# Gated-delta heads of a two-layer mixer: the next head's convolutions, sigmoids and squares inside the current head's recurrence, and output tiles that wait for their bank's readers

## The reference

```
qkv = silu(centred_dwconv(concat([qa, ka, va]), conv))    # 5 taps along the tokens
q, k = l2norm(q), l2norm(k);  g = -exp(a_log) * softplus(ga + bias);  beta = sigmoid(ba)
o_f, s_f = gdn_chunked(q, k, v, g[0], beta[0], s0[:, 0])              # forward
o_b, s_b = gdn_chunked(flip(q), ..., beta[1], s0[:, 1])               # backward
out = rmsnorm(o_f + flip(o_b)) * silu(za)

gdn_chunked:  t = inverse(I + strict_lower(kb @ k.T * decay))         # per chunk
              u = t @ vb;  w = t @ (kb * exp(g))
step over chunks:  v_new = u - w @ s;  o = q_dec @ s + (q @ k.T * decay) @ v_new
                   s = s * exp(g_last) + k_dec.T @ v_new
```

## Time and profile before

| | us |
|---|---|
| median of three runs | 3170.83 |
| lowest and highest run | 3168.66, 3173.48 |
| the profiled execution, its own time | 3164.74 |
| its span in the trace | 3162.8 |
| PE, DVE, ACT, POOL busy in the span | 2956.2, 1602.9, 821.4, 2083.2 |

### The profile page before, as it was taken

The page is one execution under the profiler, slowest core; times in us unless marked ns, Lnnn a source line. Parts: engine busy times, 40 slices in busy tenths (PEclk is TensorE's granted clock), DMA queues, the critical chain, the costliest instruction groups (busy, mean ns, idle before and its releaser), DMA issues. The chain is left out here.

```text
span 3162.8 us, 63199 instructions
## 1 busy us (share of the span) xinstructions
PE 2956.2 (93%) x26338; PEld 2742.0 (87%) x26338; DVE 1602.9 (51%) x3166; ACT 821.4 (26%) x1666; POOL 2083.2 (66%) x2491
## 2 busy tenths in 40 slices
PE   7999989999999999999979989989999999999996
PEld 2698879899999988889968888979999998887996
DVE  1655665556664534457654755673665511444112
ACT  2432334211112223320043442332111222333000
POOL 4475455477778774458857555455777888453886
PEclk9999999999999999999989999999999999999998
DMA  9421121144553421135531211122554322112223
GB/s 406 155 87 53 39 67 64 37 127 135 147 136 120 148 86 42 41 136 174 188 137 62 67 61 51 42 66 76 147 147 126 94 73 70 47 47 70 82 75 116
DMA packets 112558, 319.82 MB, mean 101 GB/s; under 512 B 16976, under 2 KB 30416, under 8 KB 111120
## 3 DMA queue, kind: packets, MB, share of 16 engines
q1 hardware_dynamic: 81536, 263.38, 26.4%
q10 hardware_dynamic: 30736, 52.40, 4.8%
HBM read 302.65 MB, written 13.08 MB: 100 GB/s over the span
## 5 line engine op out<-in xcount | busy, mean ns | idle before, releaser
L556 POOL TENSOR_SCALAR w_hi<-raw 128x256 fp32r<-128x256 f32 x1216 | 1067.4, 903 | 1009.7 <-PE projection L663 531.6
L563 POOL TENSOR_TENSOR w_lo<-raw,w_hi 128x256 fp32r<-128x256 f32 x1232 | 965.6, 814 | 6.3 <-ACT w_hi L1185 6.3
L661 PE MATMUL projection<-h_hi,w_hi 128*128 128x320 f32 x2304 | 741.8, 322 | 10.4 <-POOLq L568 4.5
L662 PE MATMUL projection<-h_lo,w_hi 128*128 128x320 f32 x2304 | 712.8, 309 | 1.1 <-issue 1.1
L663 PE MATMUL projection<-h_hi,w_lo 128*128 128x320 f32 x2304 | 712.8, 309 | 0.0
L603 PE MATMUL projection<-h_hi,w_hi 128*128 128x320 f32 x1984 | 618.5, 312 | 22.4 <-POOLq L568 20.0
L605 PE MATMUL projection<-h_hi,w_lo 128*128 128x320 f32 x1984 | 613.7, 309 | 0.0
L604 PE MATMUL projection<-h_lo,w_hi 128*128 128x320 f32 x1984 | 613.5, 309 | 0.0
L661 PEld LDWEIGHTS projection<-h_hi,w_hi 128*128 128x128 f32 x2304 | 435.3, 189 | 17.9 <-issue 9.1
L662 PEld LDWEIGHTS projection<-h_lo,w_hi 128*128 128x128 f32 x2304 | 435.4, 189 | 1.6 <-issue 1.6
L663 PEld LDWEIGHTS projection<-h_hi,w_lo 128*128 128x128 f32 x2304 | 434.4, 189 | 0.0
(11 more groups left out here) (411 smaller groups left out, 4402.9 us busy)
## 6 DMA issues: line engine op xcount, KB each, us to landing
raw<-in_w_stream SPq DMA_DIRECT2D x308, 512.0 KB, 3.6
mod_weights<-in_w_mod SPq DMA_DIRECT2D x160, 384.0 KB, 3.1
work<-in_w_ada SPq DMA_DIRECT2D x37, 512.0 KB, 6.8
work<-rows ACTq DMA_DIRECT2D x32, 320.0 KB, 4.6
xo<-rows ACTq DMA_DIRECT2D x32, 320.0 KB, 5.0
aux<-in_w_ada SPq DMA_DIRECT2D x18, 512.0 KB, 6.8
xo<-in_x ACTq DMA_DIRECT2D x1, 5120.0 KB, 18.1
work<-in_x ACTq DMA_DIRECT2D x16, 320.0 KB, 4.9
```

What stands on the lines that cost most here:

```text
L556: nc.gpsimd.tensor_scalar(w_hi[:, s, cs, :], raw[:, s, cs, :], 1.0, None, ALU.mult).then_inc(split_part, 1)
L563: nc.gpsimd.tensor_tensor(w_lo[:, s, cs, :], raw[:, s, cs, :], w_hi[:, s, cs, :].bitcast(F32), ALU.subtract).then_inc(split_part, 1)
L661: mm(o, w_hi[:, half, c, :], h_hi[:, k, hs], start=(k == 0), stop=False)
L662: mm(o, w_hi[:, half, c, :], h_lo[:, k, hs], start=False, stop=False)
```

## The change

The front of a head gets a stage of its own, `s_frt`, with its own semaphores: F is the front of the head at work, G that of the next one. PE, ACT and DVE issue parts of G inside the current head's recurrence. For the first head of a layer the front stands ahead of the head as before, with k first instead of q. "k sum" of the next head now stands between the last state products and "o sum"; "q sum" behind "k turned"; v is turned in `wb`. `pads` move into `aux`, a buffer that no other work uses by then, and `convs` and the squares to other rows of `work`. The taps read their weights in the parameters, and the copy of them (`hcw`) goes. Bodies of all but the last head of a layer end with `B.leave`, which waits for nothing. Five of a head's six input loads are issued in the head before, behind the square of o; that of `row_beta[0]` behind "q rstd". The takes of the first two tiles move behind the column scaling, z's sigmoid behind the decays, and "z ready" behind the masks' products. The numbers of cells come from `GDN_CELLS`, its first row for the first head of a layer, its second for the other three; what is left of the 64 follows "o sum". In the output projection the second tile waits for "taken1" of the turn before instead of "begun". The core of the diff:

```diff
+GDN_CELLS = ((3, 1, 2, 1, 1, 2, 2, 1, 2, 1, 1, 2), (0, 1, 2, 1, 2, 7, 2, 2, 3, 2, 2, 2))
...
-        pads = [flat(9, PADW), flat(11, PADW), flat(13, PADW)]
-        convs = [flat(15, CONVW), flat(10, CONVW, xo), flat(7, CONVW)]
+        pads = [aux[:, i * PADW:(i + 1) * PADW] for i in range(3)]
+        convs = [flat(2, CONVW), flat(6, CONVW), flat(6, CONVW)]
+        Q_SQ, K_SQ, O_SQ = wt(13), wt(15), wt(14)
...
+        s_frt = stage("gdn_front")
...
+                        if k == 0 and j < 2 and self.before:
+                            self.before.wait("act", f"ahead taken{j + 2}")
...
-                    ahead.cells(16)
-                    B.wait("act", "q squared")
-                    B.did(column_sums(wa, wt(9)), "q sum")
-                    ahead.cells(1)
-                    B.wait("act", "k squared")
-                    B.did(column_sums(wb, wt(11)), "k sum")
-                    ahead.cells(4)
-                    B.wait("dve", "k normed")
+                    if h == 0:
+                        ahead.cells(16)
+                        F.wait("act", "k squared")
+                        F.did(column_sums(wb, K_SQ), "k sum")
+                    ahead.cells(gaps[0])
+                    F.wait("dve", "k normed")
                     B.did(transposed(wb, wt(1)), "k turned")
-                    ahead.cells(2)
-                    B.wait("dve", "v silu")
-                    B.wait("act", "q rstd")
-                    B.did(transposed(wa, wt(4)), "v turned")
-                    ahead.cells(2)
+                    ahead.cells(gaps[1])
+                    F.wait("act", "q squared")
+                    if before:
+                        before.wait("act", "o rstd")
+                    F.did(column_sums(wa, Q_SQ), "q sum")
+                    F.leave()
+                    ahead.cells(gaps[2])
+                    F.wait("dve", "v silu")
+                    B.wait("act", "k turned taken")
+                    B.did(transposed(wb, wt(3)), "v turned")
+                    ahead.cells(gaps[3])
+                    F.wait("act", "q rstd")
+                    B.did(each_tile(wa, wt(1), wt(1)), "kk")
+                    ahead.cells(gaps[4])
                     B.wait("act", "v turned taken")
-                    B.did(each_tile(wa, wt(1), wt(1)), "kk")
-                    B.wait("dve", "q normed")
+                    F.wait("dve", "q normed")
                     B.did(each_tile(wb, wt(1), wt(0)), "qk")
-                    ahead.cells(9)
+                    ahead.cells(gaps[5])
...
-                        ahead.cells(1)
+                        ahead.cells(gaps[11])
+                    ahead.cells(2)
+                    B.wait("dve", f"o taken1{TILES - 1}")
+                    if G:
+                        G.wait("act", "k squared")
+                        G.did(column_sums(wb, K_SQ), "k sum")
+                    ahead.cells(1)
+                    B.wait("dve", f"o taken0{TILES - 1}")
+                    B.wait("act", "o squared")
+                    B.did(column_sums(wa, O_SQ), "o sum")
                     ahead.finish()
...
-                    B.wait("dve", "begun")
+                    if before:
+                        before.wait("dve", "taken1")
...
+                def head_inputs(h):
+                    for d in range(2):
+                        act.dma_start(gdn_state(d), io["state_gdn"][l, d, h, :, :]).then_inc(state_in[d], 16)
+                        row(h, d, row_g[d], 0, rows_in)
+                    row(h, 1, row_beta[1], 1, beta_in)
...
+                    rsqrt(F, Q_RSTD, wa[:, 0:TOK], Q_RSTD, 1.0, "q rstd", DK_SCALE)
+                    F.wait("dve", "v silu")
+                    F.leave()
+                    row(h, 0, row_beta[0], 1, beta_in)
...
+                        if n == 2:
+                            take(B, n0_, 2, xt(6))
+                        if G and n == 2:
+                            conv_sigmoid(G, 1)
+                        if G and n == 3:
+                            B.wait("act", "ahead taken2")
+                            padded(G, 2)
+                            squared_of(G, 1)
+                        if G and n == 4:
+                            conv_sigmoid(G, 0)
+                    B.wait("dve", "o whole")
+                    B.did(A(O_SQ, wt(4), ACT.Square), "o squared")
+                    if G:
+                        head_inputs(h + 1)
+                        G.wait("pe", "k sum")
+                        rsqrt(G, K_RSTD, wb[:, 0:TOK], K_RSTD, 1.0, "k rstd")
+                    B.wait("pe", "o sum")
+                    rsqrt(B, O_RSTD, wa[:, 0:TOK], O_RSTD, 1.0 / P, "o rstd")
+                    if G:
+                        conv_sigmoid(G, 2)
+                        squared_of(G, 0)
+                    B.wait("dve", "z ready")
                     take(B, n0_, 3, xt(7))
...
+                        if d == 0:
+                            F.wait("act", "q rstd")
+                            F.did(tt(wt(0), wt(0), Q_RSTD, ALU.mult), "q normed")
+                            F.leave()
...
+                        dve.wait_ge(beta_in[d], (l * H_A + h + 1) * 16)
...
+                    B.wait("act", "z sigmoid")
+                    B.link(tt(xt(8), xt(7), xt(9), ALU.mult), "z ready")
+                    if G:
+                        zeros(G)
...
+                        if G and n == 0:
+                            B.wait("pe", "wT1")
+                            taps(G, h + 1, 1, range(0, 3))
+                        if G and n == 1:
+                            taps(G, h + 1, 1, range(3, CONV_K))
+                            B.wait("act", "kdec1")
+                            taps(G, h + 1, 0, range(0, 1))
+                        if G and n == 2:
+                            taps(G, h + 1, 0, range(1, 4))
+                        if G and n == 3:
+                            taps(G, h + 1, 0, range(4, CONV_K))
+                            silu(G, 1, wt(1))
+                            taps(G, h + 1, 2, range(0, 1))
                     B.did(V.memset(cst[:, 2:3], 0.0), "o whole")
+                    if G:
+                        taps(G, h + 1, 2, range(1, CONV_K))
+                        silu(G, 0, wt(0))
+                        k_normed(G)
                     B.wait("act", "o rstd")
...
+                    if G:
+                        silu(G, 2, wt(3))
+                        B.leave()
```

More of the change, by code:

```diff
@@ L826, in _ @@
                                   f"ld{d}{v}")
-                        ahead.cells(1)
+                        ahead.cells(gaps[6])
                         for d in range(2):
@@ L852, in _ @@
                         B.did(each_tile((wa, wb)[d], KBG[d], INV_T[d]), f"wT{d}")
-                    ahead.cells(2)
+                    ahead.cells(gaps[10])
                     B.wait("act", "vb1")
@@ L1133, in _ @@
                     B.leave()
+                    before = B
                 B = s_res.body("pe", pe, l)
@@ L1275, in _, with padded, conv_sigmoid, squared_of @@
                 B.end()
+                def padded(F, i):
+                    F.wait("dve", "zeros")
+                    F.did(A(pads[i][:, 2:2 + CTX], xt(4 + i)[:, 0:CTX], ACT.Copy))
+                    F.did(A(pads[i][:, 6 + CTX:6 + TOK], xt(4 + i)[:, CTX:TOK], ACT.Copy), f"{'qkv'[i]} padded")
+                def conv_sigmoid(F, i):
+                    F.wait("dve", f"{'qkv'[i]} conv")
+                    sigmoid(F, pads[i][:, 0:CONVW], convs[i], f"{'qkv'[i]} sigmoid")
+                def squared_of(F, i):
+                    F.wait("dve", f"{'qk'[i]} silu")
+                    F.did(A((Q_SQ, K_SQ)[i], wt(i), ACT.Square), f"{'qk'[i]} squared")
@@ L1278, in _ @@
+                padded(F, 0)
+                padded(F, 1)
+                head_inputs(0)
+                conv_sigmoid(F, 1)
+                padded(F, 2)
+                squared_of(F, 1)
+                conv_sigmoid(F, 0)
+                F.wait("pe", "k sum")
+                rsqrt(F, K_RSTD, wb[:, 0:TOK], K_RSTD, 1.0, "k rstd")
+                conv_sigmoid(F, 2)
+                squared_of(F, 0)
+                before = None
                 for h in range(0, H_A):
                     B = s_gdn.body("act", act, l * H_A + h)
-                    now = int((l * H_A + h + 1) * 16)
+                    G = s_frt.body("act", act, l * H_A + h + 1) if h + 1 < H_A else None
@@ L1289, in _ @@
-                    for tile, kind in ((row_g[0], 0), (row_beta[0], 1)):
-                        act.dma_start(tile, rows[kind, bass.ds(h, 1), :].partition_broadcast(P)).then_inc(rows_in[0], 16)
-                    for i in range(2):
-                        B.wait("dve", f"{'qk'[i]} conv")
-                        sigmoid(B, pads[i][:, 0:CONVW], convs[i], f"{'qk'[i]} sigmoid")
-                        if i == 0:
-                            sigmoid(B, xt(9), xt(7), "z sigmoid")
-                    B.wait("dve", "q silu")
@@ L1297, in _ @@
```

(31 more changed lines are left out.)

149 lines of the change are left out of this document (76 added, 73 removed).

## The result

The changed kernel takes **3126.91 us** in the median of four runs (3123.91 to 3131.30), the kernel before 3172.12 beside it (3168.66 to 3173.48): a ratio of 0.9864, 95% interval 0.985 to 0.9878. The profiled executions stand 40.8 us apart (3164.74 and 3123.91), with a span of 3122.3 after. The forecast was 3145, a gain of 26: the sign and the whole range (3118 to 3168) held, the size did not, and the forecast's own range (3131 to 3159) was left at its fast end.

A forecast was written before the change was run, and what follows sets the result against it. PE was taken as the bound, with 85.5 us in eight GDN heads not work; 59 would remain, a gain of 26: 3138.7 us profiled, 3145 as median. Range 3118 to 3168, the forecast's own 3131 to 3159.

The forecast's parts named there:

- left alone: PE idle time in the GDN heads, mostly issue in the block products, that the change would not touch: 29.4 us.
- masks, all heads: PE waiting for DVE's masks before the first block product: 0.6 us in later heads, 6 in each layer's first.
- k normed and k's square in the first heads: Front of a layer's first head: PE stalls 1.9 us for k normed.
- copy of v_new for the fifth step: Recurrence: ACT's copy comes 0.7 us late, behind k's silu and square, in three heads of a layer.
- k normed and q's square in the second heads: Counted as for any later head: k normed hidden with 2.7 us to spare, q's square hidden by 0.5.
- ends of the fourth heads: End of a layer's fourth head: PE finishes its cells and waits 1.1 us for the last take.
- the forecast's clock: PE's clock falling behind the long mask stall in a layer's first head: 2 us added for each.
- rival 3: Larger gain: block-product issue idle shrinks by a third, first heads wait 2 us without a clock fall: 3123; chance 0.20.
- q stall: PE's wait for ACT's square before q's sum, 3.9 us each, would go in six heads.
- o stall: PE's 1.5 us wait for ACT's square before o's sum would go in six heads.
- Rival 1: DVE bounds the recurrence because moved taps wait for POOL, 1.7 us a tap: slower, 3187 us; chance 0.10.
- Rival 2: The stall only moves to the masks in every head, 3.6 us instead of 0.6: 3175, no change; chance 0.13.

The follow-up runs named there:

- experiment 1: Changed kernel with ten cells of each later head moved from the block levels to ahead of the masks: 3158.12 us, 0.9963 of the kernel before.
- experiment 2: Kernel before, front unmoved, with four cells a block level instead of two, taken from ahead of the masks and behind the blocks: 3201.32 us, ratio 1.0103.
- experiment 9: Kernel of experiment 8 with two cells a recurrence step, the freed cells in the block levels, and k squared behind the fifth step's copies: 3094.26 us.
- experiment 7: Changed kernel with two cells a recurrence step instead of three, except in a layer's first head; five cells go ahead of the masks: 3121.41 us.
- experiment 8: Changed kernel; z product and zeros behind first block level, first heads' five cells ahead of masks with early take, q squared before v's sigmoid: 3114.64, then 3110.32 us.

## Why the prediction was right, and where it was not

The bound and the place were right: all but 0.7 us of the change is idle time and busy time in the GDN heads. The sum, term by term, over both layers:

| term | forecast us | measured us |
|---|---|---|
| left alone (issue and small waits) | 29.4 | 13.9 |
| masks, all heads | 3.6 + 12 | 17.2 |
| k normed and k's square in the first heads | 3.8 | 3.5 |
| copy of v_new for the fifth step | 4.2 | 0 |
| k normed and q's square in the second heads | 0 | 6.1 |
| ends of the fourth heads | 2.2 | 1.9 |
| busy time over 98.8 a head (the forecast's clock) | 4 | 3.2 |
| sum | 59.2 | 45.8 |

The waits are those shown, with 0.4 us for k's square in one first head from the same view; the 4.4 for k normed (line L699) are 0.53 and 2.57 in the two first heads and 0.63 in each second one. The last term is 793.6 less 8 x 98.8. "Left alone" is the rest of the 42.6 us: 8.5 issue, 3.9 in the whole-tile levels, which no term of the forecast held, and 1.5 of small waits. The 17.2 for the masks hold the 4.0 of the second direction; its 3.0 before lay in the 29.4.

**The step that failed** is "29.4 left alone": mostly issue in the block products "which the change leaves alone", and its other form, "the cells moved into blocks and levels only space them", costed at nothing. With the spacing, issue fell by 16 us (24.6 to 8.5), more than the 13 by which the sum missed. Experiments 1, 2 and 9 show it from both sides. The other 5 of the 18 us between 3145 and 3126.91 are some 1.5 of rounding and of time outside the heads, and the step from the profiled execution to the median, put at 6.3 and measured as 3.0. The row that could have told me stood in the earlier trace rows: issue waits of up to 2.6 us lay in the densest stretch of small products, and I named no cause for them, so what four cells between them would do entered only as a chance: it is in rival 3, as a third less, 10 us, at 0.20.

**Right.** The q stall and the o stall are gone from six heads save where a second head lacks cells. The first heads' 6 us for the masks came at 5.88 and 4.38, the later heads' 0.6 at 0.75 in four of six, with 0.71 more in each for the second direction, which I had not counted. The step of the recurrence is 4.86 (4.85 forecast). The ends cost 0.9 each (1.1). The output tiles cost nothing. The second and third heads are 99 to 104 us long from one "q sum" to the next (103 to 105 forecast); that the shorter ones owe it to the issue time is argued, not shown head by head. The clock fell round the first heads' stall.

**Wrong in size.** The copy of v_new was to be 0.7 us late; it ended in time, but only just. In the fifth step ACT's first copy runs to 496.44 by its row, the second to 496.60, and PE begins at 496.55, without idle time, with the product that needs the first. No row stood behind the 0.3 us that the forecast adds for a semaphore; with two cells a step, where PE does wait (0.89, experiment 7), it begins 0.05 us after the end of the copy:

```profile
496.18 0.26 ACT L1400 ACTIVATE work<-wa 128x128 f32<-128x128 f32 x1
496.33 0.27 ACT L1400 ACTIVATE xo<-wb 128x128 f32<-128x128 f32 x1
...
496.55 0.43 PE L897 MATMUL wa<-work 128*128 128x128 f32 x2
```

```profile
495.51 0.26 ACT L1400 ACTIVATE work<-wa 128x128 f32<-128x128 f32 x1
...
495.82 0.49 PE L897 MATMUL wa<-work 128*128 128x128 f32 x2 [0.89 <-ACT work L1400]
```

**Missed.** I counted four cells behind "o sum" for every later head. A layer's first head spends all its 64 cells earlier and leaves none, so the second head reaches its "q sum" 3.5 us sooner, and q's square, hidden by 0.5 in my count, is late: 2.39 us in each layer. Squaring q ahead of v's sigmoid removed that wait (experiment 8). k normed, with 2.7 to spare in my count, is late by 0.63 in the same heads, which fits the same 3.5 us.

**The rivals.** Rival 1 falls: the taps after are

```profile
L1821 DVE SCALAR_TENSOR_TENSOR work<-aux,parameters,work x96: 885/903/1256, 195.4 to 2027.7; 128x644 f32<-128x644 f32 x96
```

with the median and the maximum of the earlier trace rows, though they now lie in the recurrence beside POOL, and experiment 7 leaves DVE in time even in a step of 3.97. The rule of the Trainium skill, SBUF — State Buffer, "Who interferes with whom", would have the later of the two wait out the earlier in full; no tap here took the 1.7 us of that. On POOL's side the stretch of the recurrence after (480.00 to 499.70) has 0.92 us an operation (9.20 in 10) where the earlier trace rows has 0.76; whether that is such a wait is not shown. Rival 2 holds in the first heads alone. Rival 3 gave 3123, near the result, but by two halves of which one was right: issue shrank, by two thirds and not one, while the first heads did wait 4 to 6 us and the clock did fall. That the total comes out near it is luck.

## What to carry to other kernels

Work that a serial chain no longer needs as its cover is worth as much for where it can stand next as for the wait that it leaves: cost the new place of every filler instruction, and the gaps that it breaks up. Before idle time is called left alone, find what ends it: "issue" in a dense stretch of small instructions is a resource too. And when cells are moved forward in an order, ask which later bank, take or queue they bring forward with them.

## What the runs showed of the hardware

I had not expected what the issue gaps are. One of them in the kernel before, PE in order of time, and the DMA queues in a window of 1.2 us inside it (packets, MB, share):

```profile
566.83 0.32 PE L685 MATMUL wb<-xo,work 128*32 128x32 f32 x15
569.74 0.39 PE L685 MATMUL wb<-xo,work 128*32 128x32 f32 x23 [2.60 <-issue]
```

```profile
q8 instruction: 1, 0.02, 4.9%
```

PE stops in the middle of forty equal products; a packet of the queue q8, which the profile calls an instruction queue, is under way in the gap and ends 1.29 us before PE goes on. Over its whole span this queue moves 207 packets:

```profile
q8 instruction: 207, 3.39, 0.4%
```

That is 16 KB each, and 52,676 matmuls and weight loads of the earlier trace rows make some 254 for each packet. In the trace of the kernel before, the stretches of over 0.25 us in which neither matmul nor weight load ran ahead of the block products fall into two kinds: 22, of 24.2 us in all, end 1.24 to 1.56 us after the end of such a packet; of the 16 others, the waits for the masks, one ends 1.72 us after a packet and the rest 2.6 us or more. In the changed kernel the first kind counts 10, of 8.2 us. The gap shown is the longest; in 20 of the 22 the packet had already ended when PE stopped, by up to 1.2 us, so what is common to them is the 1.24 to 1.56 us between the packet's end and PE's start. The reading is that in the block products, where packets mostly follow each other by 3.3 to 4.3 us, PE runs out of instructions, and that with cells of 0.88 us for twelve instructions between them it does so less. That the packet is the cause is inferred from these times and from experiments 1, 2 and 9, which change the spacing; no run changed the queue itself.

Such a gap costs more than its own length. Behind the one shown the granted clock is low, and so it is behind the longest that is left in the changed kernel, of 1.83 us; round the wait of 2.39 us for q's square in that kernel it is not (columns as in the earlier trace rows, the first of the kernel before, the others of the changed one):

```profile
569.70:574.00 4.30, 4.26 (x113) 3.82 (x114) 2.00 (x4) 0.00 (x0) 0.00 (x0) 0.60 0.01 4
```

```profile
1976.54 0.26 PE L692 MATMUL wb<-xo,work 128*32 128x32 f32 x4 [1.83 <-issue]
```

```profile
308.60:318.60 10.00, 9.88 (x70) 9.40 (x71) 9.24 (x18) 7.46 (x15) 2.18 (x3) 1.00 0.29 86
1976.50:1981.00 4.50, 4.46 (x23) 4.42 (x24) 3.25 (x5) 1.54 (x3) 2.21 (x3) 0.62 0.02 5
```

The Trainium skill, Runtime: NRT & Kernel Launch, "Instruction fetch mechanics", says that the sequencer fetches its instructions in blocks of 16 KiB, 256 of them, by a DMA queue of its own, and that this is mostly hidden. The size agrees with the 207 packets; hidden it was not here, at 24.2 us, and with three and two cells a group it nearly is, at 3.0.

What stays open: why some packets that follow the last by 5 us or more still leave a gap, as a few do in every kernel here, and how much of the last 19.4 us of idle time is to be had.
